# The second block's norms by halves of the tokens: adjacent units on 256 tokens, factors from transposed sums

## The reference

```python
for l in range(DEPTH_2):
    g = norm_g[l]
    f = _swiglu(_rmsnorm_2(x, g[0]), ffn_w_gate[l, 0], ffn_w_up[l, 0], ffn_w_down[l, 0])
    x = x + 0.5 * _rmsnorm_2(f, g[1])
    m = _mixer(_rmsnorm_2(x, g[2]), w_in[l], conv_w[l], pool_w[l], pool_scale[l], w_out[l])
    x = x + _rmsnorm_2(m, g[3])
    f = _swiglu(_rmsnorm_2(x, g[4]), ffn_w_gate[l, 1], ffn_w_up[l, 1], ffn_w_down[l, 1])
    x = x + 0.5 * _rmsnorm_2(f, g[5])
```

## Time and profile before

| | |
|---|---|
| median of 3 runs | 2868.88 us (2867.18 to 2875.83) |
| span of the profiled execution | 2864.1 us, some 4.8 us under the median |
| TensorE matmul busy | 2611.8 us, 91% |
| TensorE weight load busy | 2053.4 us, 72% |
| VectorE, ScalarE, GpSimd busy | 1366.7, 915.4, 1071.6 us |
| mean granted TensorE clock | 0.955 of full |

### The profile page before, as it was taken

The page is one execution under the profiler, slowest core; times in us unless marked ns, Lnnn a source line. Parts: engine busy times, 40 slices in busy tenths (PEclk is TensorE's granted clock), DMA queues, the critical chain, the costliest instruction groups (busy, mean ns, idle before and its releaser), DMA issues.

```text
span 2864.1 us, 34463 instructions
## 1 busy us (share of the span) xinstructions
PE 2611.8 (91%) x11068; PEld 2053.4 (72%) x11068; DVE 1366.7 (48%) x1956; ACT 915.4 (32%) x1265; POOL 1071.6 (37%) x436
## 2 busy tenths in 40 slices
PE   4988888999799999799799999599997999799997
PEld 2566676888678887576578888488885676588885
DVE  6887667535342232766443132532234656532233
ACT  3333333523332232443332232322233442332231
POOL 1222233444444444322344444344444222444442
PEclk8899899999899999999899999799999999999998
DMA  4111145222123222111122222122231111123231
GB/s 199 52 51 51 42 173 196 95 95 95 59 95 107 84 102 89 45 51 52 66 81 102 89 98 100 46 95 103 89 107 61 52 59 52 66 95 103 88 106 70
DMA packets 63564, 247.74 MB, mean 86 GB/s; under 512 B 7056, under 2 KB 7056, under 8 KB 62224
## 3 DMA queue, kind: packets, MB, share of 16 engines
q1 hardware_dynamic: 63504, 247.01, 24.7%
HBM read 244.89 MB, written 2.10 MB: 86 GB/s over the span
## 4 chain that ended last, share of the span: by engine, by line
PE 66%; issue 21%; DVE 6%; POOL 5%; ACT 1%; DVEq 0%; POOLq 0%; ACTq 0%
PE unit_bank L381 21%; PE unit_bank L383 21%; PE unit_bank L382 21%; POOL w_lo L332 3%; POOL arena L347 2%; PE out_bank L488 1%; DVE rstd L1116 1%; PE score L478 1%; DVE arena L1033 1%; PE score L475 1%; DVE arena L1507 1%; DVE arena L1505 1%; DVE arena L1494 0%; DVE arena L1495 0%; DVE arena L1376 0%
## 5 line engine op out<-in xcount | busy, mean ns | idle before, releaser
L332 POOL TENSOR_TENSOR w_lo<-raw,w_hi 128x1024 fp32r<-128x1024 f32 (+2 forms) x390 | 1006.0, 2581 | 1695.6 <-ACT w_hi L699 1695.6
L381 PE MATMUL unit_bank<-u_hi,w_hi 128*128 128x512 f32 x2160 | 858.5, 397 | 27.5 <-POOL w_lo L332 18.7
L382 PE MATMUL unit_bank<-u_lo,w_hi 128*128 128x512 f32 x2160 | 849.0, 393 | 0.0
L383 PE MATMUL unit_bank<-u_hi,w_lo 128*128 128x512 f32 x2160 | 848.3, 393 | 0.0
L699 ACT ACTIVATE w_hi<-raw 128x1024 fp32r<-128x1024 f32 (+2 forms) x390 | 430.0, 1105 | 1129.9 <-PE unit_bank L383 1083.3
L381 PEld LDWEIGHTS unit_bank<-u_hi,w_hi 128*128 128x128 f32 x2160 | 410.7, 190 | 140.5 <-POOL w_lo L332 27.9
L383 PEld LDWEIGHTS unit_bank<-u_hi,w_lo 128*128 128x128 f32 x2160 | 410.3, 190 | 87.2
L382 PEld LDWEIGHTS unit_bank<-u_lo,w_hi 128*128 128x128 f32 x2160 | 410.7, 190 | 85.6 <-issue 1.4
L381 PE MATMUL unit_bank<-h_hi,w_hi 128*128 128x512 f32 x992 | 390.6, 394 | 5.3 <-DVE h_lo L1566 3.6
L382 PE MATMUL unit_bank<-h_lo,w_hi 128*128 128x512 f32 x992 | 386.7, 390 | 0.0
L383 PE MATMUL unit_bank<-h_hi,w_lo 128*128 128x512 f32 x992 | 386.6, 390 | 0.0
(11 more groups left out here) (238 smaller groups left out, 2370.5 us busy)
## 6 DMA issues: line engine op xcount, KB each, us to landing
raw<-in_w_gate_up SPq DMA_DIRECT2D x176, 512.0 KB, 3.2
raw<-in_w_down SPq DMA_DIRECT2D x64, 704.0 KB, 4.0
raw<-in_w_in SPq DMA_DIRECT2D x70, 512.0 KB, 3.2
f<-in_w_ada_rows SPq DMA_DIRECT2D x32, 512.0 KB, 4.9
raw<-in_w_up SPq DMA_DIRECT2D x32, 512.0 KB, 3.3
raw<-in_w_out SPq DMA_DIRECT2D x24, 512.0 KB, 3.3
ada_w<-in_w_ada SPq DMA_DIRECT2D x8, 1024.0 KB, 7.4
raw<-in_w_down SPq DMA_DIRECT2D x16, 512.0 KB, 3.3
```

Of the source, the lines that this page charges most:

```text
L332: e.tensor_tensor(w_lo[:, s, 0:n], raw[:, s, 0:n], as32(w_hi[:, s, 0:n]), ALU.subtract).then_inc(lo_ready, 1)
L381: e.matmul(bank[:], wh, hi(k), start=n == 0, stop=False)
L382: e.matmul(bank[:], wh, lo(k), start=False, stop=False)
L383: mm = e.matmul(bank[:], wl, hi(k), start=False, stop=last)
```

## The change

Boundaries 0 to 6 are rewritten; what is computed is the same.

- The last pair of units before a norm (`last_pair`) and the first pair after it (`next_pair`) run on 256 tokens at a time: all of tokens 0 to 255, then 256 to 511. Each matmul of 512 columns becomes two of 256.
- The post norm's sums are made transposed (`f_sums`): a slice of 128 tokens of `acc`, and of the last unit's square, is the stationary operand, and a column of ones the moving one, so each token's sum stands in one column of 128 rows. Root and reciprocal then work on 2 columns, and `spread` brings the result back to all rows by a product of the broadcast column with the identity.
- The pre norm's squares are no longer added by GpSimd: `u_square` multiplies each square by a column of ones on TensorE, VectorE reduces the 32 columns.
- VectorE reads the factor from PSUM and keeps `f*g*factor` in PSUM (`unit_bank`) rather than SBUF; it updates x and makes `u_lo` for 256 tokens at a time, and takes the last pair's second half in between.
- The second pair's first unit (`next_unit`) does all its products with `w_hi` first and those with `w_lo` last, and carries the spread of the pre norm's factor.
- The layer loop is written out twice, so boundary 3 is made like the others. At boundary 0 the squares' sums move from TensorE (L407) to VectorE (`add_square`), as elsewhere.
- ScalarE's table of functions is loaded ahead of the last units instead of at the root.

```diff
+HALVES = (slice(0, T // 2), slice(T // 2, T))
+NORMS = 3 * LAYERS + 1
+F_SQUARES, F_ADDS = DC + 2, DC + 1
...
+            def last_pair(p, hi, lo, ks, r):
+                last = len(ks) - 1
+                for s in range(2):
+                    e.wait_ge(lo_ready, 2 * p + s + 1)
+                    e.wait_ge(taken[s], p + 1)
+                    for n, k in enumerate(ks):
+                        mm = three(unit_bank[s], s, k, hi(k), lo(k), HALVES[0], n == 0, n == last)
+                    mm.then_inc(part_done, 1)
+                for s in range(2):
+                    for n, k in enumerate(ks):
+                        if s == 0 and n == 4:
+                            f_sums(r, 0, out_bank)
+                        if s == 0 and n == 7:
+                            spread(r, 0, stat_bank)
+                        mm = three(mix[s], s, k, hi(k), lo(k), HALVES[1], n == 0, n == last)
+                    mm.then_inc(unit_done, 1)
+            def f_sums(r, t, bank):
+                e.wait_ge(fsq_added, F_ADDS * r + DC + t)
+                e.wait_ge(fsq_ready, F_SQUARES * r + DC + 2 * t)
+                for b, tokens in blocks(t):
+                    e.matmul(bank[:, b:b + 1], acc[:, tokens], tab("ones", 0, 1), start=True, stop=False)
+                    mm = e.matmul(bank[:, b:b + 1], sq[:, 1, tokens], tab("ones", 0, 1), start=False, stop=True)
+                mm.then_inc(sums_ready, 1)
+            def spread(r, t, bank):
+                e.wait_ge(inverse_ready, root_at(r, t))
+                for b, tokens in blocks(t) if t < 2 else blocks(0) + blocks(1):
+                    at = b if t < 2 else 4 + b
+                    mm = e.matmul(bank[:, tokens], inverse[:, at:at + 1].broadcast_to([P, P]), tab("ident"),
+                                  start=True, stop=True)
+                mm.then_inc(spread_ready, 1)
+            def u_square(m, t, c):
+                e.wait_ge(sq_ready, 2 * DC + 2 * DC * m + DC * t + c + 1)
+                for b, tokens in blocks(t):
+                    mm = e.matmul(mix[0][:, DC * b + c:DC * b + c + 1], sq[:, c % 2, tokens], tab("ones", 0, 1),
+                                  start=True, stop=True)
+                mm.then_inc(sq_used, 1)
...
+            def next_pair(p, m):
+                def u(s, t, c):
+                    return three(score[s], s, c, u_hi[:, c, :], u_lo[:, c, :], HALVES[t], c == 0, c == DC - 1)
+                e.wait_ge(lo_ready, 2 * p + 1)
+                e.wait_ge(taken[0], p + 1)
+                for c in EIGHT:
+                    e.wait_ge(u_ready, u_at(m, 0, c))
+                    u(0, 0, c)
+                    if c:
+                        u_square(m, 0, c - 1)
+                    if c == 3:
+                        f_sums(m, 1, mix[1])
+                    if c == 5:
+                        spread(m, 1, out_bank)
+                e.wait_ge(lo_ready, 2 * p + 2)
+                for c in EIGHT:
+                    u(1, 0, c)
+                    if c == 0:
+                        u_square(m, 0, DC - 1)
+                for c in range(DC + 4):
+                    if c < DC:
+                        e.wait_ge(u_ready, u_at(m, 1, c))
+                        mm = u(0, 1, c)
+                        if c == DC - 1:
+                            mm.then_inc(unit_done, 1)
+                    if c >= 4:
+                        mm = u(1, 1, c - 4)
+                    if 0 < c <= DC:
+                        u_square(m, 1, c - 1)
+                mm.then_inc(unit_done, 1)
+            def next_unit(p, s, m=None):
+                e.wait_ge(hi_ready, 2 * p + s + 1)
+                e.wait_ge(taken[s], p)
+                for k in EIGHT:
+                    if k == 3 and m is not None:
+                        spread(m, 2, stat_bank)
+                    wh = w_hi[:, s, k * P:(k + 1) * P]
+                    e.matmul(unit_bank[s][:], wh, u_hi[:, k, :], start=k == 0, stop=False)
+                    e.matmul(unit_bank[s][:], wh, u_lo[:, k, :], start=False, stop=False)
+                e.wait_ge(lo_ready, 2 * p + s + 1)
+                for k in EIGHT:
+                    mm = e.matmul(unit_bank[s][:], w_lo[:, s, k * P:(k + 1) * P], u_hi[:, k, :], start=False,
...
+            def high_part(m, t, c):
+                e.wait_ge(x_ready, x_at(m, t, c))
+                settled()
+                e.activation(u_hi[:, c, HALVES[t]], x[:, c, HALVES[t]], ACT.Identity,
+                             scale=col("norm_g", 2 * m * DC + c)).then_inc(uhi_ready, 1)
+                e.wait_ge(sq_used, 2 * DC + 2 * DC * m + DC * t + c - 1)
+                e.activation(sq[:, c % 2, HALVES[t]], x[:, c, HALVES[t]], ACT.Square).then_inc(sq_ready, 1)
...
+                for s in range(2):
+                    e.wait_ge(part_taken, 2 * r + s + 1)
+                    f_square(part, 0, s, r)
+                e.wait_ge(sums_ready, 2 * r + 1)
+                norm_root(r, 0, out_bank[:, 0:2], 0, 2)
+                highs(0, 0)
+                e.wait_ge(taken[0], p + 2)
+                f_square(part, 1, 0, r)
+                if m is not None:
+                    refill(p + 1, 0)
+                highs(0, 1, 2, 3)
+                e.wait_ge(taken[1], p + 2)
+                f_square(part, 1, 1, r)
+                if m is not None:
+                    refill(p + 1, 1)
+                highs(0, 4, 5)
+                e.wait_ge(sums_ready, 2 * r + 2)
+                norm_root(r, 1, mix[1][:, 2:4], 2, 2)
+                highs(0, 6, 7)
+                highs(1, *range(DC))
+            def u_root(m):
+                e.wait_ge(u_summed, m + 1)
+                norm_root(m, 2, u_sums, 4, 4)
+                e.wait_ge(spread_ready, root_at(m, 2))
+                e.activation(rstd[:], stat_bank[:], ACT.Copy).then_inc(rstd_ready, 1)
...
+                def chunk(n):
+                    t, c = rows[n]
+                    if c == 0:
+                        e.wait_ge(spread_ready, root_at(r, t))
+                    update(t, c, (stat_bank, out_bank)[t][:, HALVES[t]])
+                    if n and m is not None:
+                        low_part(m, *rows[n - 1])
+                def add_part(t):
+                    e.wait_ge(fsq_ready, F_SQUARES * r + DC - 1 + 2 * t)
+                    e.wait_ge(fsq_added, F_ADDS * r + DC - 1 + t)
+                    e.tensor_tensor(acc[:, HALVES[t]], acc[:, HALVES[t]], sq[:, 0, HALVES[t]],
+                                    ALU.add).then_inc(fsq_added, 1)
+                e.wait_ge(part_done, 2 * r + 1)
+                take(DC - 2, 0, unit_bank[0]).then_inc(part_taken, 1)
+                add_part(0)
+                e.wait_ge(part_done, 2 * r + 2)
+                take(DC - 1, 0, unit_bank[1]).then_inc(part_taken, 1)
+                invert_roots(r, 0, 0, 2)
+                chunk(0)
+                e.wait_ge(unit_done, 2 * p + 1)
+                take(DC - 2, 1, mix[0]).then_inc(taken[0], 1)
+                add_part(1)
+                for c in range(1, 4):
+                    chunk(c)
+                e.wait_ge(unit_done, 2 * p + 2)
+                take(DC - 1, 1, mix[1]).then_inc(taken[1], 1)
+                for c in range(4, 7):
+                    chunk(c)
+                invert_roots(r, 1, 2, 2)
+                for n in range(7, 2 * DC):
+                    chunk(n)
+                if m is not None:
+                    low_part(m, 1, DC - 1)
+                    e.wait_ge(sq_used, 2 * DC + 2 * DC * (m + 1))
+                    e.tensor_reduce(u_sums, mix[0][:, 0:4 * DC].rearrange("p (b c) -> p b c", c=DC),
+                                    mybir.AxisListType.X, ALU.add).then_inc(u_summed, 1)
+                    invert_roots(r, 2, 4, 4)
+                    e.wait_ge(rstd_ready, m + 1)
...
+            def post_norm(r):
+                def update(t, c, factor):
+                    at = (2 * r - 1) * DC + c
+                    g = col("norm_g", at) if r % 3 == 2 else half_g[:, at:at + 1]
+                    part = unit_bank[c % 2][:, HALVES[t]]
+                    step(e.scalar_tensor_tensor(part, f[:, c, HALVES[t]], g, factor, ALU.mult, ALU.mult))
+                    e.tensor_tensor(x[:, c, HALVES[t]], part, x[:, c, HALVES[t]], ALU.add).then_inc(x_ready, 1)
```

262 lines of the change are left out of this document (130 added, 132 removed).

## The result

The changed kernel takes 2879.97 us (2875.74 to 2886.76, 15 runs) where the kernel before, in turn with it on the same chip, takes 2871.88 (2866.67 to 2878.5, 15 runs): a ratio of 1.0029, 95% interval 1.002 to 1.0038. It is slower by 8 us where 14 less were forecast. The profiled executions have spans of 2873.9 and 2864.1, 9.8 apart. One of experiment 5's twelve executions took 6777 us, for a reason that nothing recorded shows; it is not in the ratio there and moves the median by 0.2.

What follows compares the result with a forecast made beforehand. Bound: seven boundaries, 250.0 us with TensorE about half busy, at most 185 open. Gains of 36.0 us at full clock less 22.5 for the fallen clock leave 13.5: 2850.6 profiled, 2855 us median; range 2828 to 2890.

Steps and rivals of the forecast that it cites:

- the first term of the sum: Last pair at boundaries 1, 3, 4: 17.2 us against 15.0, with the first half's factor at about 12.2.
- the unit behind the pair: Second pair's first unit: 3.6 us of `w_hi` products before it needs `w_lo`, which hides the 2.12 us wait.
- The pitch of narrow matmuls: Split matmuls of 256 columns: 0.12 us from start to start, with ends of 0.107 and 0.19.
- the rival of paced weight loads: Narrow split matmuls paced by weight loads: gain gone from 0.134 us on, over 2920 at 0.19; chance 0.12.
- TensorE's 7.85 and 27.36 us between the sublayers: TensorE's idle at boundaries 1 and 3, forecast to leave no idle of over 2.5 us between the two sublayers.
- The two holds of `u_lo`: Next pair, VectorE: two `w_lo` of the first new pair hold a `u_lo` for about 2.0 us each, 4.0.
- the update in PSUM: VectorE's write to PSUM: 0.41 us an operation, bounded by 0.05 less and 0.2 more.
- The ring of squares: Next pair, waits among ScalarE, TensorE and VectorE with only two square buffers: some 2 us, then 2.3 in the second half.
- It fell in the first half as forecast: Clock at 1.2 GHz from about 21 to 35 us of a boundary, costing 22.5 us in all.
- a rival of 0.25: Clock lost again in the second half: 7 us more gives 2870, without a break to 50 gives 2888; chance 0.25.
- two bounds of its own core: Forecast wrong in its core if boundary 1 gains over 6 us or loses over 3, or boundary 3 gains under 8.

Runs made afterwards that it cites:

- experiment 5: Changed kernel with the edits of 1 and 2, the second slot's 16 `w_hi` products moved into the next pair's first-half rounds, two a round: 2868.33 us, 0.9969.
- 1: Changed kernel with the products with `w_hi` first in the last pair's second slot, those with `w_lo` behind them: 2858.76 us, 0.9949 to the kernel before.
- 2: Changed kernel with four buffers of squares in place of two: 2855.93 us, 0.9939 to the kernel before.
- 9: Kernel of 6 with the second slot's 16 `w_hi` products in the first half's rounds 4 to 7, four a round: 2806.34 us, 0.9788 to the kernel before.
- 4: Kernel before, without token halves, its layer loop written out and boundary 3 interleaved like the others: 2864.95 us, 0.9966 to the kernel before.
- 7: Edits of experiment 5 and 6 together, on the changed kernel with those of 1 and 2: 2836.61 us, 0.9877 to the kernel before.
- 6: Changed kernel with the edits of 1 and 2, and `w_lo` of a slot made in four pieces: 2819.41 us, 0.9815 to the kernel before.

## Why the prediction was wrong

**The step that failed** is the first term of the sum: "Last pair: 132 x 0.12 + 8 narrow products of sums + 4 of the spread at 0.109 = 17.2", with the factor "at about 12.2". The price of a split matmul was right (0.120 from start to start), the count too. What the step left out is that halving the units also halves the time under which the second slot's `w_lo` is made. I had asked the question for the unit behind the pair, whose `w_hi` products hide 2.12 us, and not for the last pair. At after's boundary 1 the pair is 21.1 us long and the factor stands at 15.9: 2.2 of waiting and 1.5 of clock more than 12.2. Over all boundaries the wait is 15.4 us and the clock behind it some 6.0, 21.4 of the 26.7 us by which the boundaries are over the forecast. Taking it away (1) gave 21 (23 by the ratios). That settles the sign: without it the kernel is faster than before. That the two figures are so near is partly luck: in the trace of 1 the boundaries gave back 15.1, about the wait alone, and the clock was down for 137 us at six of them where after had 133. It no longer fell in the last pairs and fell longer behind them.

**What held.** The pitch of narrow matmuls, so the rival of paced weight loads is out. TensorE's 7.85 and 27.36 us between the sublayers are gone. The two holds of `u_lo` are there (2.47 and 2.28), and the update in PSUM is 0.48 + 0.42, inside its bounds. The ring of squares was priced at 26, and four buffers gave 24 (2), with some of the clock's share in it.

**The clock.** It fell in the first half as forecast, for 10 to 20.5 us where 14 were forecast, and once more at boundaries 0 and 3. At the six boundaries with a next pair it was down for 133 us in all, 14 of them in last pairs, where six times 14 would be 84: the forecast had this too small. That the second half would lose it was a rival of 0.25; that happened at two boundaries in part. Of its cost, the executions of 9 give the best measure, being of one kernel on one chip: from their mean clocks I estimate some 57 us more at 1.2 GHz in the two slower ones than in the two fastest, and they took 18 us longer. If TensorE alone set the pace, 57 us at half the clock would cost 28; so part of a slow round lies under other engines' work.

**Boundary by boundary.** The forecast named two bounds of its own core: boundary 1 losing over 3 us (it lost 3.3) and boundary 3 gaining under 8 (6.3). Both were crossed. At boundary 1 the wait and the clock behind it, 3.7 us, are enough to explain it. At boundary 3 the wait is 2.2 of the 6.0 us missed; the clock's second fall stands beside it. And without the wait (1) both are still crossed, with 62.4 and 62.6 us, by the clock that fell twice. Boundary 3's gain did come, as far as it did, from work put in order and not from halves (4).

**Still open.** Why the clock falls once at one boundary and twice at a like one: 1 shows both in one trace.

## What to carry to other kernels

Where a unit of work is cut, ask of every producer that ran beneath it whether it still has the time; the operand made one unit ahead is the first to be late. Two buffers that suffice while the engines alternate may tie three engines into a ring once one of them has a long block to run; the forecast had priced this ring, at about its size, and left it in. When an idle engine is to be filled with real work, place it where its operands have arrived: beside `w_lo` in pieces, the same 16 matmuls cost 17 us from round 0 on (7 against 6) and gave 8 to 13 from round 4 on (9 against 6), the latter only where the clock held. And where a gain comes with the clock, read the clock of every execution, not of one.

## What the hardware showed that was not expected

- A wait of 2.2 us of TensorE in a dense row of 0.12 us matmuls was followed by a granted clock of 0.50 in four of seven last pairs, though the row had begun again 1.4 us before the fall (boundary 1). In the trace of 1, without the wait, no last pair had a fall.
- A `u_lo` of 0.47 us lasts up to 2.47 us beside a GpSimd operation on 1024 columns, and up to 0.90 with GpSimd's work in pieces of 256 and 352. Cut in four, a slot costs GpSimd 3.17 against 2.39 us and the whole kernel still gains 12 to 15.
- Matmuls with 128 x 128 weights of their own and 256 columns follow each other by 0.120 us at full clock and 0.214 at half.
